# New orders for the last down turns of both feed-forward blocks, and the mixer's last turn written out

## The reference

```python
h = x + 1/2 * g1 * SwiGLU1(mod(rms(x)))
h = h + gm * Mixer(mod(rms(h)))
h = h + 1/2 * g2 * SwiGLU2(mod(rms(h)))
y = mod(rms(h))                        # final norm, shift/scale from c
# Mixer: z = xn @ w_in (six sections of 1024 columns); A: conv + RG-LRU scan, times GeLU gate;
# B: u * (lower-triangular spatial mix of layernorm(v)); out = (sig(gA)*A + sig(gB)*B) @ w_out
```

## Time and profile before

| | us |
|---|---|
| median of 3 runs | 2569.76 (2568.68 to 2570.29) |
| the profiled execution | 2574.91 |
| its span | 2573.2 |
| TensorE busy | 2437.8 (95%) |
| VectorE busy | 1665.5 (65%) |
| ScalarE busy | 1054.7 (41%) |
| mean granted TensorE clock | 0.972 |

### The profile page before, as it was taken

One profiled execution on the slowest core, in us unless ns is written; L12 is line 12 of the kernel. 1 busy time (PEld: TensorE's weight loads), 2 busy tenths in 40 slices (PEclk: granted clock), 3 DMA queues, 4 the chain that ended last, 5 costly groups with the idle time before them and its releaser, 6 DMA issues.

```text
span 2573.2 us, 32028 instructions
## 1 busy us (share of the span) xinstructions
PE 2437.8 (95%) x11514; PEld 2050.1 (80%) x11514; DVE 1665.5 (65%) x2636; ACT 1054.7 (41%) x1817; POOL 166.9 (6%) x199
## 2 busy tenths in 40 slices
PE   7899999999899989999999998968999999989997
PEld 3477777777788767999999998956777788878786
DVE  4977667666566765655566666168667657666675
ACT  2544444444333432433333444125445444433334
POOL 3000000000000000001101110110000000000000
PEclk9899999999999989999999999988999999999997
DMA  9245544556855422421222224023554543496531
GB/s 359 71 150 168 184 156 149 184 167 218 322 221 213 157 91 79 135 61 45 57 61 61 61 65 159 16 106 99 163 162 150 172 143 123 154 351 259 221 131 76
DMA packets 245119, 381.02 MB, mean 148 GB/s; under 512 B 16641, under 2 KB 158137, under 8 KB 243462
## 3 DMA queue, kind: packets, MB, share of 16 engines
q1 hardware_dynamic: 232302, 345.15, 38.5%
q0 software_dynamic: 10240, 33.56, 4.7%
q10 hardware_dynamic: 2456, 0.75, 0.1%
HBM read 262.93 MB, written 116.47 MB: 147 GB/s over the span
## 4 chain that ended last, share of the span: by engine, by line
PE 69%; DVE 16%; DMA 6%; issue 5%; ACT 3%; SPq 1%; DVEq 0%; ACTq 0%; POOL 0%
PE bank L482 20%; PE bank L483 20%; PE bank L484 20%; DVE u_lo L559 3%; DMA h_dram<-stage_lo 3%; DMA wraw<-in_w_ffn_down 2%; PE bank L2552 1%; PE bank L2550 1%; PE bank L2553 1%; DVE stage_lo L1794 1%; DVE wraw L586 1%; PE bank L2461 1%; DVE ada_lo L1809 1%; PE bank L2568 1%; DVE h L1802 1%
## 5 line engine op out<-in xcount | busy, mean ns | idle before, releaser
L482 PE MATMUL bank<-ops,u_hi 128*128 128x512 f32 x1232 | 490.6, 398 | 21.6 <-ACT g L1153 10.9
L559 DVE TENSOR_TENSOR u_lo<-wraw,u_hi 128x512 fp32r<-128x512 f32 (+2 forms) x532 | 317.5, 618 | 287.6 <-ACT u_hi L553 284.8
L483 PE MATMUL bank<-ops,u_hi 128*128 128x512 f32 x1232 | 487.1, 395 | 0.0
L484 PE MATMUL bank<-ops,u_lo 128*128 128x512 f32 x1232 | 485.9, 394 | 0.0
L482 PE MATMUL bank<-xn_hi,w_hi 128*128 128x384 f32 x1152 | 387.9, 337 | 15.7 <-DVE xn_lo L2343 9.7
L553 ACT ACTIVATE u_hi<-wraw 128x512 fp32r<-128x512 f32 (+2 forms) x532 | 289.6, 567 | 261.9 <-PE bank L484 167.7
L483 PE MATMUL bank<-xn_lo,w_hi 128*128 128x384 f32 x1152 | 385.7, 335 | 0.0
L484 PE MATMUL bank<-xn_hi,w_lo 128*128 128x384 f32 x1152 | 385.6, 335 | 0.0
L482 PEld LDWEIGHTS bank<-ops,u_hi 128*128 128x128 f32 x1232 | 235.2, 191 | 85.8 <-ACT g L1153 12.5
L484 PEld LDWEIGHTS bank<-ops,u_lo 128*128 128x128 f32 x1232 | 235.0, 191 | 51.3
L483 PEld LDWEIGHTS bank<-ops,u_hi 128*128 128x128 f32 x1232 | 235.6, 191 | 49.8
(11 more groups left out here) (305 smaller groups left out, 4242.9 us busy)
## 6 DMA issues: line engine op xcount, KB each, us to landing
h_dram<-stage_hi SPq DMA_DIRECT2D x154, 256.0 KB, 2.4
h_dram<-stage_lo SPq DMA_DIRECT2D x154, 256.0 KB, 2.7
ada_raw<-in_w_ada POOLq DMA_DIRECT2D x96, 256.0 KB, 3.1
raw<-in_w_in SPq DMA_DIRECT2D x48, 512.0 KB, 4.7
wraw<-in_w_ffn_gate SPq DMA_DIRECT2D x44, 512.0 KB, 3.8
wraw<-in_w_ffn_up SPq DMA_DIRECT2D x44, 512.0 KB, 4.8
wraw<-in_w_ffn_down SPq DMA_DIRECT2D x48, 384.0 KB, 5.4
x<-x_dram SPq DMA_DIRECT2D x6, 2304.0 KB, 11.9
```

The source lines that it names most:

```text
L482: nc.tensor.matmul(out, hi, mov_hi, start=first, stop=False, skip_group_check=True)
L483: nc.tensor.matmul(out, hi, mov_lo, start=False, stop=False, skip_group_check=True)
L484: return nc.tensor.matmul(out, lo, mov_hi, start=False, stop=last, skip_group_check=True)
L559: nc.vector.tensor_tensor(unit(u_lo, u, n), unit_source(u, n), unit(u_hi, u, n).bitcast(F32), ALU.subtract).then_inc(u_lo_ready, 1)
```

## The change

It touches four places.

- The last turn of FFN1 gets an order of its own (`last_of_first` on each engine). TensorE: A11, samples, S2, samples, transpose, A12, S3, transpose, A22, S1, sums of half 0, S4[0], spread, S4[1]. S3 and S4 use ring places 6 and 7. The squares are all added by VectorE, so the sums read one operand per half. The statistics of the samples come second and those of half 1 third; the v projection takes tiles 4, 5 and 6 together, and ScalarE empties bank 0 for tile 6 between two normalised tiles.
- The last turn of FFN2 gets another order (`last_of_second`): A11, samples, S1, S2, samples, transpose, A12, transpose, S3, A22, sums of the samples, S4[0], spread of the samples, S4[1], sums of half 0. The samples' rows are normalised before the outputs of half 0.
- In FFN2's turn 0 the second round of shift transposes and its copy move behind S3.
- The mixer's loop has 7 turns on ScalarE and VectorE, and the eighth is written out (`mix(KT - 1, True)`): the splits of the merged tiles 0 to 5 stand between its steps, tile 0 in three parts of 384 columns. The reload of the first half of x moves behind the last merged tile, and TensorE waits per tile and per third.

The core of the diff, in the order SyncE, ScalarE, VectorE, TensorE:

```diff
+RANK = ((1, 2, 3), (1, 3, 2), (1, 2, 3), (2, 3, 1))
+LAST_UPDATES = ("W0 W1 F0 F1 V0 X0 X1 Y0 Y1 Z0 Z1 S0 S1 V1".split(),
+                "Y0 Y1 S0 S1 W0 W1 F0 F1 V0 V1 X0 X1 Z0 Z1".split())
...
-                if k == 4:
-                    sp.dma_start(x[:, 0:KH, :], x_dram[:, 0:KH, :]).then_inc(x_back, 16)
                 sp.dma_start(merged_in[k][:, :], merged_dram[k]).then_inc(merged_back[k], 16)
-            sp.wait_ge(m_lo_ready, KT)
+            sp.dma_start(x[:, 0:KH, :], x_dram[:, 0:KH, :]).then_inc(x_back, 16)
+            sp.wait_ge(m_lo_ready, merged_count(KT - 1))
+            sp.wait_ge(x_back, 16)
...
+                        squares(1, 6, 8)
+                        snap_down(2, 0, E_P7[0], 7)
+                        squares(1, 8, 9)
+                        snap_down(2, 1, E_P7[1], 8)
+                        squares(1, 9, 10)
+                        unit_hi(act, f, g, 14)
+                        unit_hi(act, f, g, 15)
+                        v_split(0, E_K1[1])
+                        squares(1, 10, 12)
+                        root(1, 0)
...
+                        for k in range(KH):
+                            scaled(0, k)
+                        snap_down(2, 0, E_P7[0], 7)
+                        squares(3, 8, 9)
+                        snap_down(2, 1, E_P7[1], 8)
+                        squares(3, 9, 10)
...
+                    elif k == 3:
                         v_split(2, E_K1[1])
+                        root(i, 2)
...
+                nc.scalar.activation(nstd[:, 13:14], epst[:, 0:1], ACT.Gelu_apprx_tanh)
+                normalised(1, 0)
+                act.wait_ge(x_spilled, 16 * 2)
+                act.wait_ge(v_mm, 1)
+                nc.scalar.activation(v_all[:, 0, 0:HALF], bank[0][:, :], ACT.Gelu_apprx_tanh).then_inc(act_evicted, 1)
...
+                for c in pieces_:
+                    cols = slice(c * width, (c + 1) * width)
+                    nc.scalar.activation(xn_hi[:, k, cols], merged_in[k][:, cols], ACT.Copy).then_inc(m_hi_ready, 1)
...
+                        if ends and s == 1 and c == NCH - 1:
+                            merged_hi(0)
                         evicts(18 + 3 * s + c, sig[:, c, :], bank[3 + c][:, 0:CH], ACT.Sigmoid)
+                    if ends and s == 1:
+                        merged_hi(1)
+                        merged_hi(2)
...
+                        add_squares(1, 6, 8)
+                        dve.wait_ge(x_written, written - XW_ROUND)
+                        w_part(0)
+                        w_part(1)
+                        f_part(0)
+                        f_part(1)
+                        add_squares(1, 8, 9)
+                        v_part(0)
+                        add_squares(1, 9, 10)
+                        x_part(0)
+                        x_part(1)
+                        add_squares(1, 10, 12)
+                        unit_lo(dve, f, g, 14)
+                        unit_lo(dve, f, g, 15)
+                        v_split(0, E_K1[1])
+                        reciprocal(1, 0)
+                        y_part(0)
+                        normalised(0, 0)
+                        y_part(1)
+                        normalised(0, 1)
+                        z_part(0)
+                        normalised(0, 2)
+                        v_split(1, E_P4[1])
+                        sample_update(1)
+                        normalised(0, 3)
+                        normalised(0, 4)
+                        v_split(2, E_P5[1])
+                        normalised(0, 5)
+                        z_part(1)
+                        s_part(0)
+                        normalised(0, 6)
+                        reciprocal(1, 2)
+                        s_part(1)
+                        v_split(3, E_P3[1])
+                        normalised(0, 7)
+                        v_part(1)
+                        add_squares(1, 12, 15)
+                        normalised(0, 8)
+                        add_squares(1, 15, 16)
+                        sample_rows()
+                        reciprocal(1, 1)
+                        for k in range(KT + 1):
+                            normalised(1, k)
...
+                        y_part(0)
+                        y_part(1)
+                        unit_lo(dve, f, g, 14)
+                        unit_lo(dve, f, g, 15)
+                        s_part(0)
+                        s_part(1)
+                        sample_update(0)
+                        add_squares(3, 6, 8)
+                        w_part(0)
+                        w_part(1)
+                        f_part(0)
+                        f_part(1)
+                        sample_update(1)
+                        v_part(0)
+                        v_part(1)
+                        add_squares(3, 8, 9)
+                        x_part(0)
+                        x_part(1)
+                        add_squares(3, 9, 10)
+                        reciprocal(3, 2)
+                        z_part(0)
+                        z_part(1)
+                        sample_rows()
+                        reciprocal(3, 0)
...
+                if ends:
+                    merged_lo(0)
+                    merged_lo(1)
                 for b in range(NS):
...
+                if ends:
+                    merged_lo(2)
...
                 nc.vector.tensor_tensor(gg[:, :], gg[:, :], qn[:, :], ALU.mult).then_inc(merge_step, 1)
+                if ends:
+                    merged_lo(3)
...
                 nc.vector.tensor_tensor(merged[:, :], gg[:, :], ug[:, :], ALU.add).then_inc(merged_ready, 1)
+                if ends:
+                    merged_lo(4)
+                    merged_lo(5)
...
+            def half_sums(i, c):
+                pe.wait_ge(xs_written, i + c)
+                last = max(p for p in range(NSQ) if SQUARES[i][p][0] == c)
+                pe.wait_ge(acc_added, added(i, last + 1))
+                pe.wait_ge(squared, i * NSQ + last + 1)
+                row_sums(i, c, [acc[i][:, c, :]] + [tsq[p] for p in range(NSQ) if SQUARES[i][p][0] == c and SQUARES[i][p][2]],
+                         True, True)
...
+                        samples_down(1)
+                        turn_rows(0)
+                        loaded(O_B21)
+                        tile(A12[0], O_B21, W[0], True, True)
+                        tile(A12[1], O_B21, W[1], True, True)
...
+                        turn_rows(1)
+                        loaded(O_T4)
+                        pe.wait_ge(snapped, snaps(f, g, 5))
+                        tile(A22[0], O_T4, X[0], False, True)
...
+                        tile(S1[1], O_T1, Z[1], True, False)
+                        half_sums(1, 0)
+                        loaded(O_B22)
+                        pe.wait_ge(x_written, last_update(0, "Y0"))
+                        tile(S4[0], O_B22, Z[0], False, True)
+                        spread(1, 0)
+                        pe.wait_ge(x_written, last_update(0, "Y1"))
+                        tile(S4[1], O_B22, Z[1], False, True)
...
+                        tile(A22[1], O_T4, X[1], False, True)
+                        sample_sums(3)
+                        loaded(O_B22)
+                        pe.wait_ge(x_written, last_update(1, "Y0"))
+                        tile(S4[0], O_B22, Z[0], False, True)
+                        spread(3, 2)
+                        pe.wait_ge(x_written, last_update(1, "Y1"))
+                        tile(S4[1], O_B22, Z[1], False, True)
+                        half_sums(3, 0)
...
+                        shift_turn(0)
...
                     tile(S3[1], O_T3, X[1], False, False)
+                    if f == 1 and rho == 0:
+                        shift_turn(1)
...
+                for t in ((0, 2, 3, 1) if k == 0 else range(4)):
+                    if k == 0 and t == 1:
+                        pe.wait_ge(x_written, last_update(0, "Z0"))
+                    if k == KT - 1 and t == 2:
+                        spread(1, 1)
                     v_step(0, t, k)
                 if k == 3:
-                    early_sums(1, 1)
-                    late_sums(1, 1)
+                    sample_sums(1)
                 elif k == 5:
-                    spread(1, 1)
-            sample_sums(1)
-            pe.wait_ge(x_written, XW_FFN1)
+                    spread(1, 2)
+                elif k == 6:
+                    half_sums(1, 1)
+            pe.wait_ge(x_written, last_update(0, "Z1"))
+            pe.wait_ge(samples_act, 2)
             for k in range(KT):
                 pe.wait_ge(xn_lo_ready, KT + k + 1)
-                for t in (4, 5):
+                for t in (4, 5, 6):
+                    if k == 0 and t == 6:
+                        pe.wait_ge(act_evicted, 1)
                     v_step(0, t, k)
-            spread(1, 2)
-            for t in (6, 7, 8):
+            for t in (7, 8):
...
+                                pe.wait_ge(m_lo_ready, merged_count(0, c))
+                                if o == 1:
```

(13 more changed lines are left out.)

528 lines of the change are left out of this document (302 added, 226 removed).

## The result

The changed kernel takes 2537.15 us (median of 4 runs, 2533.23 to 2538.47), the kernel before 2570.03 beside it: a ratio of 0.987, interval 0.9847 to 0.9892. That is 32.9 us less where I forecast 24.4. The direction was right. By the ratio the time is 2536.4 us, just under the low end of my range (2537).

What follows compares the result with a forecast made beforehand. TensorE, busy 95% of the span, bounds the kernel; only its pauses, small products and low clock can give time. -12.5 - 9.1 + 0.7 - 3.5 = -24.4 us off the 2569.76 median: 2545.4 us, range 2537 to 2557.

Steps and rivals of the forecast that it cites:

- B: End of the mixer: projection starts 7.95 us earlier and its slow products go; -9.1 us (-7.5 to -10).
- C: Shift rows in FFN2's first down turn: nothing gained past slot H, a slow stretch may become visible; +0.7 us (0 to +2.5).
- A: End of FFN1 and the v projection: new order with fewer sums and pauses; -12.5 us (-8 to -17).
- Step (5): V projection: from tile 4's low half VectorE sets the pace, 16.8 us; the second half starts at 940.1.
- Step (6): V projection's second half: three looped tiles, bank 0 emptied early, evictions free from 952.0, 8.7 us pause gone; 13.8 us.
- D: End of FFN2 and the output: early part later, fewer records and pauses afterwards; -3.5 us (-7 to 0).
- an earlier fall of the clock: Closing stage: the clock was expected to fall near 2530, 12 us earlier than before, costing 4 us more.
- The stores end the kernel as before: Kernel's end: VectorE's last eight rows (5.46 us) and the stores were to end it as before.
- The clock holds: Rival: thin work doesn't drop the clock; A -16, D -7, C 0, so -32, 2538 us; chance 0.14.
- The round trips: Slower rival: TensorE's seven waits on queued VectorE work cost 4.7 us more each, all seven 2578 us; chance 0.04.
- VectorE was not later than counted: Rival that VectorE is later than counted: A -8, B -7.5, D -1, so -16, 2554 us; chance 0.15.
- two signs of being wrong: Seam behind FFN1: VectorE idle while TensorE waits over 2 us in one piece, or low clock over 12 us.

Runs made afterwards that it cites:

- experiment 5: Kernel after, with the eight squares of FFN1's last turn read by TensorE's sums again instead of added by VectorE: 2547.01 us.
- experiment 3: Kernel after, with two tiles instead of three in the v projection's second loop and bank 0 emptied with the other banks: 2539.08 us.
- kernel 2: Kernel after, with both rounds of FFN2's shift transposes ahead of S3 again: 2537.16 us.
- experiment 7: Kernel after, with seven unread products put into the 2.8 us pause ahead of the last A22 tile in FFN2's last turn: 2536.34 us.
- experiment 9: Kernel after, with VectorE's three passes over the sample rows moved behind tile 3's rows in the closing stage: 2539.99 us.

## Why the prediction was right or wrong

**B held, term by term.** I predicted a wait of 1.75 us behind the last product, it is 1.78; the clock stays at its upper level (none of the 27.4 us low, 10.2 before); the written-out turn starts without a gap. The pause of 0.9 at k = 2 didn't come. -9.7 for -9.1. The clock there isn't certain: three other traces of the new order have 3.4 us of low clock and 28.6 us.

**C held in its sum.** The gain in front is given back, and -0.2 was measured for +0.7. The pauses are others than I had them. The first, on the snapshot behind the stores, is 1.63 us for 3.2. The second is 5.20 for 5, but it waits for slot F (issued at 2260.25, landed 15.5 us later) ahead of the first A22 tile, and not for a snapshot. The wait for slot H was to be longer than 0.9 us, and is 0.36. The +0.7 stood for a slow stretch on visible products; the stage has 3.4 to 6.8 us of low clock now and had 6.8 in each trace of before.

**A: near the size, with one step led by the wrong reason.** Set against the start of the stage (the after is 1.0 us later there), the instants came out: stall of 1.8 at 883.9 (1.9 at 882.9 + 1.0 predicted), 1.0 ahead of A22[1] (1.0), the two waits of 1.5 for 1.8 and 1.6, 1.75 for 1.9 at tile 4. TensorE's timeline of the after:

```profile
883.94 0.49 PE L2731 MATMUL bank<-u_hi,hs_in 128*128 128x512 f32 x1 [1.77 <-DVE u_lo L588]
...
898.78 1.02 PE L2649 MATMUL bank<-ones,acc 128*128 128x1 f32 x8
901.31 0.47 PE L498 MATMUL bank<-slotE,u_hi 128*128 128x512 f32 x1 [1.51 <-issue]
...
921.12 0.80 PE L498 MATMUL bank<-w_hi,xn_hi 128*128 128x512 f32 x1 [1.75 <-DVE xn_lo L2303]
```

Step (5) held: VectorE sets the pace from tile 4's low half on (experiment 5), over 17.8 us for 16.8, and the second half started 2.2 us ahead of its 940.1 + 1.0. Step (6) adds 12.2 us of its 13.8 and leads with the third tile and bank 0, which carry 1 to 2 (experiment 3). The rest comes from the samples' low half, finished 3.3 us ahead of my 952.0 + 1.0. No kernel here takes back the order of the samples' statistics by itself, so its share is read from the rows. Against the four traces of before the seam gained 10.9, not the 15.8 that the first pair alone shows: that trace of before was its slowest.

**D failed, and this is the error of the forecast.** The early part is as predicted: TensorE ends the sums of half 0 28.5 us after the stage's start, before it stood there at 24.7, 3.8 us later for 3.9. From there to VectorE's last row I expected 11.1 us less by the work (3.7) and the pauses (7.4), and 4 more for an earlier fall of the clock: 7.1 in all. (With the 3.9 that is -3.2, not the -3.5 that stands there.) The traces show 36.5 before and 21.3 after, 15.2 less. The windows of both kernels (length, busy us and instructions of TensorE, weight loads, VectorE, ScalarE, GpSimd; clock), for that whole part and for its slow stretch, before and then after:

```profile
2533.50:2573.20 39.70, 26.08 (x138) 24.64 (x136) 17.68 (x25) 7.43 (x14) 0.00 (x0) 0.64 0.31 123
2538.40:2565.40 27.00, 21.53 (x99) 20.72 (x100) 9.02 (x13) 6.02 (x11) 0.00 (x0) 0.50 0.23 89
```

```profile
2508.90:2535.30 26.40, 17.90 (x121) 17.51 (x121) 13.20 (x20) 4.42 (x9) 0.00 (x0) 0.73 0.48 185
2514.10:2524.40 10.30, 9.38 (x46) 9.32 (x46) 3.08 (x5) 2.23 (x5) 0.00 (x0) 0.50 0.37 135
```

The pauses went as I had them: 8.4 us before and 0.9 after. The work didn't. TensorE's busy time there fell from 26.08 to 17.90, 8.2 us less, where my two terms made it 0.3 more. I had counted only the 17 records fewer, at the slow 0.22 us, as if all that remain were as slow as before, and then added 4 us for a fall near 2530. In fact the low stretch held 99 records of 27 us before and holds 46 of 10.3 now.

That fall isn't certain either way. The pause of 2.8 us came in every trace. In the first trace of after the clock stayed up behind it; in the other two it fell right there, at 17 to 21 us from the stage's start, and the slower products were absorbed by the wait behind them: the sums of half 0 end 28.4 us from the start in both. In kernel 2, with the same order, it fell for 10.2 us from 18.4 on, and the stage took 58.5 us, 4.1 more than the mean of the after. So the 4 us came in one of nine traces with this order, and I had put them into the forecast as the rule. Why the clock stays up longer in the new order is open: it may be the waits of 2.9, 1.0 and 4.5 us that are gone, but filling the one at A22[1] (experiment 7) changed nothing for the better, and putting back the 4.5 (experiment 9) left 17.1 us of low clock, about as without it. No kernel here takes back the order of FFN2's last turn by itself.

The second thing that I left out goes the other way. "The stores end the kernel as before" was wrong: the nine stores of 512 KB come closer together, and the last byte lands 5.15 us behind VectorE's last row (6.35 and 5.8 in the other two traces), 3.1 in all four of before. SyncE's queue in the after:

```profile
2520.31 3.08 SPq L993 DMA_DIRECT2D out_y_prompt<-yrow  x4
2524.62 0.33 SPq L993 DMA_DIRECT2D out_y_sample<-yrow  x1
2526.23 4.28 SPq L993 DMA_DIRECT2D out_y_prompt<-yrow  x4
```

In slices of 1.9 us the core moved 398 to 411 GB/s from 2522.5 to 2531.9; VectorE made its last eight rows from 2524.8 to 2530.2. 3.8 - 15.2 + 2.0 = -9.4, the 9.5 us of these two traces.

**The rivals.** "The clock holds" (0.14) came nearest: 2538 against 2537.15. Its D was -7, and its A -16 was not needed. The round trips were priced right near 1.8 us each (1.0 to 1.8, one 2.8). VectorE was not later than counted. Of my two signs of being wrong the first didn't come (no wait of TensorE in the seam over 1.77 us), and the second, over 12 us of low clock there, came in one of the three traces (17.1). The range was too narrow below: its low end stood 1 us under the middle of that rival, with no room for an error in the rival's own terms, and D's came to be 4 us past the -7 that I had given as its end.

## What to carry to other kernels

One-column sums that TensorE needs for a norm at a seam are on the chain of everything behind them. Here 64 records were worth 7 us, though part of the additions that replaced them lies on VectorE's own chain, and 48 more, with earlier stores, another 6. Before pricing two waits in a row, ask whether they hang on one queue: then the second takes what the first gives. An instruction that waits for another engine (a root behind sums) belongs behind the work that doesn't need it, and its price is the wait, not its length. A fall of the clock that comes in some executions belongs into the range of a forecast, with a chance, and not into its sum. Before a forecast, compare more than one trace of the kernel before where its clock is not steady.

## What the runs showed of the hardware

Low stretches of the clock are no fixed property of a place: the same instructions of the seam had 10.2 to 27.3 us of it in four executions, the unchanged stage of FFN2 0 to 6.8, and there each 3.4 us of it cost about 2. The end of before is steadier, with 28.3 us or more in all four. The same instructions of the new closing stage had 14.4 to 18.1 us of it in eight traces and 26.5 in the ninth. And nine stores close together moved at about 400 GB/s, and the end came 4.6 to 6.5 us behind the last row in these nine, where it came 3.1 behind it before.
